# A hybrid recurrence/attention backbone on one Trainium2 core: the projection of the recurrence layers starts by groups of tokens

## The reference, cut to what matters

```python
def _centred_shift(h):                       # half the sum of both neighbours
    prev = pad(h[:, :-1]); nxt = pad(h[:, 1:])
    return 0.5 * (prev + nxt)
...
xx = concatenate([_centred_shift(hc), _centred_shift(hx)], axis=1) - h
xs = h[None] + xx[None] * mu[:, None, None, :]              # six mixtures
r, k, v, g = einsum("nbtd,nde->nbte", xs[:4], w_rkvg)       # four 1024 x 1024 projections
dec_lora = ... tanh(xs[4] @ w1) @ w2 ; iclr from xs[5] in the same way
```

## Time and profile before

| what | us |
|---|---|
| median of three runs (7787.57 to 7800.44) | 7795.02 |
| the profiled execution, its own time | 7794.21 |
| its span, first to last instruction | 7792.3 |
| PE busy | 6080.1 (78%) |
| DVE busy | 3070.1 (39%) |
| ACT busy | 2020.2 (26%) |
| POOL busy | 1540.3 (20%) |

### The profile page before, as it was taken

One profiled execution on the slowest core, in us unless ns is written; L12 is line 12 of the kernel. 1 busy time (PEld: TensorE's weight loads), 2 busy tenths in 40 slices (PEclk: granted clock), 3 DMA queues, 4 the chain that ended last, 5 costly groups with the idle time before them and its releaser, 6 DMA issues. The chain is left out here.

```text
span 7792.3 us, 214350 instructions
## 1 busy us (share of the span) xinstructions
PE 6080.1 (78%) x91872; PEld 4135.5 (53%) x91872; DVE 3070.1 (39%) x6989; ACT 2020.2 (26%) x3486; POOL 1540.3 (20%) x1838
## 2 busy tenths in 40 slices
PE   5999777777777999788796441769699877777777
PEld 4555666666663554455443331544355566666664
DVE  3101555555551331455101788111310355555552
ACT  1000344344431111343111220210100244444440
POOL 1450222222220541000064000000000122222220
PEclk8999988888988999898998555579799988888989
DMA  3222000000003221321222233132111100000001
GB/s 107 88 94 72 24 16 16 17 22 16 16 13 117 89 88 50 91 61 39 91 100 77 48 44 35 48 77 82 69 67 67 46 16 16 16 16 16 16 16 65
DMA packets 172658, 401.96 MB, mean 52 GB/s; under 512 B 18752, under 2 KB 89280, under 8 KB 172224
## 3 DMA queue, kind: packets, MB, share of 16 engines
q1 hardware_dynamic: 137472, 297.39, 13.7%
q10 hardware_dynamic: 34752, 98.58, 3.1%
HBM read 286.86 MB, written 109.05 MB: 51 GB/s over the span
## 5 line engine op out<-in xcount | busy, mean ns | idle before, releaser
L316 PE MATMUL ps<-arena 128*128 128x512 f32 (+1 forms) x5824 | 2137.1, 529 | 262.6 <-DVE arena L1531 132.7
L316 PEld LDWEIGHTS ps<-arena 128*128 128x128 f32 x5824 | 1107.6, 191 | 1284.4 <-issue 1235.1
L1706 PE MATMUL ps<-arena 64*64 64x64 f32 x35840 | 731.1, 223 | 143.1 <-issue 60.3
L1706 PEld LDWEIGHTS ps<-arena 64*64 64x64 f32 x35840 | 635.4, 135 | 225.9 <-issue 209.5
L150 POOL TENSOR_TENSOR arena<-arena 128x512 f32<-128x512 f32 (+1 forms) x360 | 327.6, 927 | 1828.0 <-DMA arena<-w_mod 1817.7
L1973 ACT COPY arena<-ps 128x512 f32<-128x512 f32 (+1 forms) x880 | 537.1, 630 | 506.3 <-PE ps L1706 497.5
L530 PE MATMUL ps<-arena 128*128 128x512 f32 (+1 forms) x1152 | 424.6, 529 | 40.0 <-DMA arena<-na_w_in 40.0
L2071 POOL TENSOR_TENSOR arena<-arena 128x256 f32<-128x256 f32 (+1 forms) x320 | 276.9, 871 | 876.8 <-DVE arena L2209 438.6
L2027 POOL MEMSET arena<- 128x1024 f32 (+1 forms) x6 | 4.2, 739 | 2108.9 <-issue 2108.9
L1531 DVE SCALAR_TENSOR_TENSOR arena<-arena 128x1280 f32<-128x1280 f32 x96 | 150.5, 1641 | 633.0 <-PE ps L316 632.0
L153 POOL TENSOR_TENSOR arena<-arena 128x256 f32<-128x256 f32 (+2 forms) x504 | 380.2, 766 | 51.2
(11 more groups left out here) (249 smaller groups left out, 9858.5 us busy)
## 6 DMA issues: line engine op xcount, KB each, us to landing
proj<-arena ACTq DMA_DIRECT2D x104, 640.0 KB, 3.9
arena<-proj SPq DMA_DIRECT2D x104, 640.0 KB, 5.1
arena<-w_mod SPq DMA_DIRECT2D x96, 512.0 KB, 5.8
arena<-rw_w SPq DMA_DIRECT2D x68, 512.0 KB, 3.5
arena<-xres SPq DMA_DIRECT2D x40, 640.0 KB, 6.9
xres<-arena ACTq DMA_DIRECT2D x24, 640.0 KB, 6.6
arena<-na_w_in SPq DMA_DIRECT2D x24, 512.0 KB, 3.8
arena<-x SPq DMA_DIRECT2D x16, 640.0 KB, 6.7
```

What stands on the lines that cost most here:

```text
L316: last = nc.tensor.matmul(k.ps[:, 3 * u + n, 0:b - a], w[:, c * P:(c + 1) * P], src[:, c, a:b], start=(c == 0), stop=(c == KT - 1))
L1706: last = PE.matmul(part_of(out, dst, hh, g, d), part(l, src, hh, g, d), rhs, start=True, stop=True)
```

## The change

VectorE does the sums, the edge copies, the differences and mixture 0 for tokens 0-512, then for 512-1024, then for 1024-1280, and raises a new semaphore `xs_part` after each. TensorE's first projection has a wait for the matching group ahead of the matmuls of each chunk, in each strip; `xs_ready` now counts from mixture 1 on. TensorE's filling is one `hold` shorter in either recurrence layer.

```diff
-NORM_FILL = {0: 154, 3: 72}
+NORM_FILL = {0: 153, 3: 71}
...
-        xs_ready = sem("xs_ready")
+        xs_ready, xs_part = sem("xs_ready"), sem("xs_part")
...
-            for c in range(KT):
-                V.tensor_tensor(dd[:, c, 1:T - 1], h[:, c, 0:T - 2], h[:, c, 2:T], ALU.add)
-            dve.drain()
-            for a, b in SEGS:
-                V.tensor_copy(dd[:, :, a:a + 1], h[:, :, a + 1:a + 2])
-                V.tensor_copy(dd[:, :, b - 1:b], h[:, :, b - 2:b - 1])
-            dve.drain()
-            for c in range(KT):
-                V.scalar_tensor_tensor(dd[:, c, :], dd[:, c, :], 0.5, h[:, c, :], ALU.mult, ALU.subtract)
-            dve.drain()
-            for n in range(6):
+            def mix(n, c, a, b):
+                return V.scalar_tensor_tensor(xs[n % 2][:, c, a:b], dd[:, c, a:b], k.mu[:, (j * 6 + n) * KT + c:(j * 6 + n) * KT + c + 1],
+                                              h[:, c, a:b], ALU.mult, ALU.add)
+
+            edges = [t for a, b in SEGS for t in ((a, a + 1), (b - 1, b - 2))]
+            for a, b in CHUNKS:
+                lo, hi = max(a, 1), min(b, T - 1)
+                for c in range(KT):
+                    V.tensor_tensor(dd[:, c, lo:hi], h[:, c, lo - 1:hi - 1], h[:, c, lo + 1:hi + 1], ALU.add)
+                dve.drain()
+                for t, beside in edges:
+                    if a <= t < b:
+                        V.tensor_copy(dd[:, :, t:t + 1], h[:, :, beside:beside + 1])
+                dve.drain()
+                for c in range(KT):
+                    V.scalar_tensor_tensor(dd[:, c, a:b], dd[:, c, a:b], 0.5, h[:, c, a:b], ALU.mult, ALU.subtract)
+                dve.drain()
+                for c in range(KT):
+                    last = mix(0, c, a, b)
+                last.then_inc(xs_part, 1)
+            for n in range(1, 6):
...
                 for c in range(KT):
-                    last = V.scalar_tensor_tensor(xs[n % 2][:, c, :], ...)
+                    last = mix(n, c, 0, T)
                 last.then_inc(xs_ready, 1)
...
             for n in range(4):
-                pe.wait_ge(xs_ready, n + 1)
+                if n:
+                    pe.wait_ge(xs_ready, n)
                 with pe.Fori(0, 4) as i:
                     for u in range(2):
                         pe.wait_ge(w_in[u], i * 16 + (64 * n + 16))
                         pe.wait_ge(ev_done[u], i + 4 * n + 1)
-                        strip_matmuls(nc, k, u, strips_[:, u, :], xs[n % 2]).then_inc(mm_done[u], 1)
+                        if n:
+                            strip_matmuls(nc, k, u, strips_[:, u, :], xs[n % 2]).then_inc(mm_done[u], 1)
+                        else:
+                            for m, (a, b) in enumerate(CHUNKS):
+                                pe.wait_ge(xs_part, m + 1)
+                                for c in range(KT):
+                                    last = nc.tensor.matmul(k.ps[:, 3 * u + m, 0:b - a], strips_[:, u, c * P:(c + 1) * P], xs[0][:, c, a:b],
+                                                            start=(c == 0), stop=(c == KT - 1))
+                            last.then_inc(mm_done[u], 1)
...
-                pe.wait_ge(xs_ready, 5 + u)
+                pe.wait_ge(xs_ready, 4 + u)
```

More of the change, by code:

```diff
@@ L1530, in _ @@
                 for c in range(KT):
-                    last = V.scalar_tensor_tensor(xs[n % 2][:, c, :], dd[:, c, :], k.mu[:, (j * 6 + n) * KT + c:(j * 6 + n) * KT + c + 1],
-                                                  h[:, c, :], ALU.mult, ALU.add)
+                    last = mix(n, c, 0, T)
                 last.then_inc(xs_ready, 1)
```

## The result

The changed kernel takes 7754.4 us in the median of five runs (7741.66 to 7761.21); the kernel before, run beside it, 7791.8. The ratio is 0.9949, with a 95% interval of 0.9936 to 0.9962: 40 us less, between 30 and 50. Forecast was 7753, from a gain of 41.5 us. The profiled execution of the changed kernel is one of the faster (7743.64), so its span has shrunk by more (7792.3 to 7741.8, 50.5 us) than the runs' 40; what follows goes by stretches, not by spans.

What follows compares the result with a forecast made beforehand. TensorE's wait for VectorE's mixtures before each recurrence layer's projection, and VectorE's loop refetches, were taken as the bounds. Start 18 us plus jumps 23.5 made 41.5 off 7794.2, so 7752.7, run median 7753; range 7744 to 7781.

Steps and rivals of the forecast that it cites:

- The start, layer 3: Layer 3's first projection: TensorE starts on VectorE's first group, so strip 1 ends 11 us earlier, 10 after the clock allowance.
- the clock: TensorE's first strip: low clock after the two pauses, bounded between 0 and about 3 us a layer, taken as 1 each.
- The start, layer 0: Layer 0's first projection: strip 1 ends at 224.5 against 233.5, 9 us earlier, 8 after the clock allowance.
- VectorE's loop in layer 0: Layer 0's recurrence: loop moved by 54 spans three blocks, is no longer fetched again; seven jumps' waits fall by 23.5 us.
- four blocks stay: VectorE's instruction fetch: it holds four blocks of 128, three of the loop and one fetched ahead; low end 0 if not.
- The other reading, two lines: VectorE's instruction fetch: two 16 KiB lines, so the 344-instruction loop is fetched again wherever it lies; only 18 us won.
- Layer 3's loop: Layer 3's recurrence: VectorE's loop moved by 108 still spans four blocks, so 25 us of waits and five packets stay.
- The rival with TensorE's loop: TensorE's inner loop of 1,712 instructions slips over a block limit: 64 jumps cost 237 us, total 7990; chance 0.05.

Runs made afterwards that it cites:

- place probe: Kernel before with 88 idle VectorE instructions in layer 0's norm and 96 in layer 3's; one run, 7773.62 us, 11 below before.
- the shift alone: Kernel before with 54 idle VectorE instructions at the head of each recurrence layer's norm, no grouping; ratio 0.9979 to the kernel before.
- the interleaved order: Changed kernel with TensorE's first projection ordered by chunk, then by strip; ratio 0.9928 to the kernel before, 56 us below it.

## Why the prediction was right

**The start, layer 3: right but for the clock.** The third group was set at 40.9 us and came at 40.3; strip 1 was set at 61.6 and came at 61.3. The clock was set at 1 us on top, and cost nothing here. Windows of TensorE around its second pause show what there is of it (length; busy and count of PE, PEld, DVE, ACT, POOL; granted clock; DMA share, GB/s):

```profile
5516.10:5519.50 3.40, 3.40 (x5) 1.61 (x6) 3.24 (x11) 0.00 (x0) 0.00 (x0) 0.56 0.00 0
5519.50:5524.70 5.20, 5.19 (x13) 1.95 (x11) 5.12 (x14) 0.00 (x0) 0.00 (x0) 1.00 0.00 0
5525.20:5546.20 21.00, 20.96 (x65) 12.38 (x66) 11.69 (x8) 1.23 (x1) 0.00 (x0) 1.00 0.15 56
```

After 5.88 us of idleness the clock is at 0.56 (1.00 in the 2.9 us of chunk 0 before it), mostly the lower level of 1.2 GHz, and chunk 1 takes 8.59 us instead of 6.9; but the third group comes later than that. After the pause of 0.54 us it is at 1.00, so chunk 2 and strip 1 lost nothing.

**The start, layer 0: a term too small.** I let VectorE's added work stretch to 6.5 us; it became 8.3 (51.7 was set for the third group, 53.5 came), and 6.2 us were won instead of 8. The clock's 1 us is in this: chunk 1 began at 195.28 after a pause of 14.07 us, at 0.50 of full speed, and was through 1 us after the third group was ready.

The stretch was taken as a share of the time. It is one by the piece. From 161.63 to 189.84 us VectorE runs 24 instructions, one to each of the 24 of GpSimd's turn, in 28.2 us; the same 24 take 15.3 in layer 3, so each lost 0.54 us. Before, 16 instructions of 1,280 columns stood beside GpSimd ahead of TensorE's start at 197, 31.9 us instead of 23.1, and each lost 0.55. What the loss follows is GpSimd's instruction and not VectorE's: in the traces a VectorE instruction lasts about 0.2 us longer beside a GpSimd one of 128 columns, 0.4 to 0.5 beside 256, 0.8 to 1.1 beside 512, whether its own columns are 512 or 1,280. Cut into more pieces, VectorE's work met all 24 of GpSimd's instructions before the third group was ready, and not only two thirds of them. The Trainium skill (SBUF — State Buffer, section SBUF: two separate sides) calls the port pair of the two engines an exclusive lock held for a whole instruction, which agrees with this alternation; had I used it, I would have priced the instructions and not the columns. It doesn't give the order in which the lock is handed on, and GpSimd's 11.82 us behind eight instructions of VectorE, above, is not an alternation. GpSimd gains by the smaller pieces too: its first turn ended at about 189 instead of 207.6.

**VectorE's loop in layer 0: the mechanism right, its size 3 us too large.** Seven jumps now cost 4.4 us, not the 1.4 I had left them: 0.63 each. The waits fell by 20.5 us instead of 23.5. A loop that stays still pays for its jump, more than other short gaps. That four blocks stay (three of the loop and the one fetched ahead) was a choice between rows that left it open; the runs bear it out: loops starting in my estimate at 10 to 22, 1 to 16 and 17 to 32 places into a block stay, those at 44 to 56, 69 to 84 and 84 to 104 don't. The other reading, two lines, under which no place helps, is out.

**Layer 2's loop: a term left out.** I counted places for the recurrences only. The state-space loop moved as well and costs 4.2 us more, in all eight kernels that have the shift of 54 in layer 0 (305.8 to 306.2 us, against 301.9 and 301.6 in the two that have the old place and 303.3 in the place probe).

**Layer 3's loop, and TensorE's.** Both as said: 25.6 us and five packets a tile stay in layer 3, and q8's packets are 298 before and after. The rival with TensorE's loop didn't come to pass; that a single instruction would have tipped it was not tried.

**The total: closer than its terms.** The terms as measured are 6.2 + 11.5 + 20.5 - 4.2 = 34.0 us, where the forecast had 41.5 and the runs say 40, between 30 and 50. The mechanisms were right, but that 7753 and 7754.4 lie 1.4 us apart is luck: a start in layer 0 and a loop priced 2 and 3 us too high and 4.2 us overlooked in layer 2 stand against a TensorE that ran faster in the recurrences than the waits explain.

**TensorE's clock in the recurrences.** Layer 0's recurrence with the residual behind it, from its first instruction to the next layer's first product, fell from 1729.2 to 1701.0 us in the two profiles: 28.2, of which the waits explain 20.5. The windows of just this stretch, before and after (length; busy and count of PE, PEld, DVE, ACT, POOL; granted clock; DMA share, GB/s):

```profile
803.09:2532.30 1729.21, 1333.33 (x38369) 1085.27 (x38369) 880.72 (x1571) 646.58 (x1034) 416.81 (x480) 0.88 0.08 28
...
795.55:2496.60 1701.05, 1308.91 (x38369) 1058.05 (x38369) 879.77 (x1571) 645.82 (x1034) 416.27 (x480) 0.89 0.08 28
```

VectorE, ScalarE and GpSimd are busy as long as before, to 1 us. TensorE's matmuls, the same number, take 24.4 us less at a somewhat higher granted clock. The eleven profiles split in the same way, in both layers. Where VectorE's loop stays, the stretch takes 1680.6 to 1701.0 us in layer 0 (TensorE busy 1293 to 1309) and, counted to the end of the kernel, 1614.8 to 1619.7 in layer 3 (1254 to 1264). Where it doesn't, it takes 1719.0 to 1729.2 (1316 to 1333) and 1635.8 to 1652.4 (1271 to 1289). So a loop that is fetched again goes with a slower TensorE, beyond its own waits; I had this term at nothing.

**What stays open.** How the jump's wait and the clock hang together was not tried. Within either group the stretch still scatters by 5 to 20 us, while the projections of one kind scatter by less than 2. By the runs the shift alone is worth 16 us (9 to 23), no more than its waits; the terms of the profiles, one execution each, can't be added to the runs' gain more finely than that.

## What to carry to other kernels

An edit that adds instructions moves every loop behind it. Before crediting a gain or a loss to the edit, look at the idle time before the first instruction of later loops and at the packets of the instruction queues, and try the old kernel with as many idle instructions: here 16 of 40 us came from there (11 of 37 by medians), and placing the second loop as well brought some 20 to 27 more. When a consumer is fed in pieces, order its work so that each piece feeds all that it can (the interleaved order gave another 16 us), and where two engines take turns at a port, price the turns by their number and by the other engine's instructions, not by your own columns.

## What the runs showed of the hardware

- VectorE's instructions come in packets of 8 KB, 128 instructions. A loop of 344 that, by my count of places, lies in three such blocks is brought once and a jump costs 0.6 us; in four, it is brought again at each turn, five packets and 3.6 us a jump. In one kernel, with the loop's end some 4 to 16 instructions inside the fourth block, it was 6.1 us.
- VectorE and GpSimd, both with two operands from SBUF, mostly take turns by the instruction: 0.54 us more for each of 24 VectorE instructions of 512 columns, 0.55 for each of 16 of 1,280, by the size of GpSimd's instruction and not of VectorE's. In one stretch they didn't: a GpSimd multiplication lasted 11.82 us while eight instructions of VectorE went ahead at their usual 1.55.
- A pause of 5.88 us brought TensorE's granted clock from 1.00 down to 0.56, one of 0.54 us did not. In the recurrences the same matmuls took some 1.5% to 2% more busy time, on average over the profiles, where VectorE's loop was fetched again.
